# The attention layer's modulation, moved into the phase that reads out and projects the recurrence

## The reference

```python
for i in range(DEPTH_2):                                    # two layers
    last = i == DEPTH_2 - 1
    mod_x = jax.nn.silu(c) @ mod_w[i] + mod_b[i]            # [1024] @ [1024, 3072]
    mod_c = jax.nn.silu(c_ctx) @ mod_w[i] + mod_b[i]
    sh_x, sc_x, g_x = jnp.split(mod_x[:, None, :], 3, axis=-1)
    sh_c, sc_c, g_c = jnp.split(mod_c, 3, axis=-1)
    h_x = rmsnorm_2(x, norm_g[i]) * (1.0 + sc_x) + sh_x
    h_c = rmsnorm_2(ctx, norm_g[i]) * (1.0 + sc_c) + sh_c
    ...                                                     # i = 0: recurrence; i = 1: attention
    x = x + g_x * d_x
    if not last:
        ctx = ctx + g_c * d_c
```

## Time and profile before

| | us |
|---|---|
| median of three runs | 3451.7 (3448.46 to 3469.91) |
| profiled execution, own time | 3456.56 |
| its span in the trace | 3454.8 |
| TensorE busy | 2627.6 (76% of the span) |
| VectorE busy | 1449.8 (42%) |
| ScalarE busy | 705.3 (20%) |
| GpSimd busy | 499.7 (14%) |

### The profile page before, as it was taken

How to read it: one execution, slowest core, us unless ns; L and a number is a source line. 1 busy time by engine, 2 the same in 40 slices (tenths; PEclk the granted TensorE clock), 3 DMA queues, 4 the chain that set the end, 5 groups by cost and what they waited for, 6 DMA issues and landing times. The chain is left out here.

```text
span 3454.8 us, 49188 instructions
## 1 busy us (share of the span) xinstructions
PE 2627.6 (76%) x19847; PEld 1493.6 (43%) x19847; DVE 1449.8 (42%) x2794; ACT 705.3 (20%) x1317; POOL 499.7 (14%) x469
## 2 busy tenths in 40 slices
PE   5998853975777778766059999778885877888876
PEld 2542333934322333222035565367774325444542
DVE  1634666524211111111578796845554801134431
ACT  2111420101100000000025541122222112133330
POOL 0000141300211111111000000021111210044440
PEclk7999876986899989888579999989997988999998
DMA  5104501014599999888534546243433442011002
GB/s 208 67 32 146 195 8 25 6 49 162 184 415 410 414 403 415 346 336 335 226 89 124 152 123 207 75 113 112 115 104 129 159 147 81 13 23 19 8 1 79
DMA packets 337449, 540.07 MB, mean 156 GB/s; under 512 B 151685, under 2 KB 225311, under 8 KB 304081
## 3 DMA queue, kind: packets, MB, share of 16 engines
q1 hardware_dynamic: 306657, 436.31, 35.7%
q10 hardware_dynamic: 17568, 75.51, 5.4%
q0 software_dynamic: 13008, 25.20, 2.0%
HBM read 481.30 MB, written 75.02 MB: 161 GB/s over the span
## 5 line engine op out<-in xcount | busy, mean ns | idle before, releaser
L1812 PE MATMUL psum<-ex_w,hT 128*64 128x512 f32 x1344 | 348.4, 677 | 109.8 <-DMA ex_w<-in_exp_w_up 103.8
L1812 PEld LDWEIGHTS psum<-ex_w,hT 128*64 128x64 f32 x1344 | 120.0, 156 | 333.6 <-issue 325.2
L3692 POOL TENSOR_SCALAR at_p<-at_p,at_stats 128x768 f32<-128x768 f32 x64 | 139.8, 2207 | 200.8 <-DVE at_stats L3717 200.8
L533 PE MATMUL psum<-hT,weights 128*128 128x512 f32 x384 | 166.8, 592 | 0.0
L2027 DVE COPY slot_act_t<-psum 128x256 f32<-128x256 f32 x32 | 13.6, 424 | 355.0 <-PE psum L1820 355.0
L1828 PE MATMUL psum<-ex_w,slot_act_t 128*64 128x512 f32 x672 | 153.5, 598 | 7.6 <-DVE slot_act_t L2173 6.4
L234 PE MATMUL psum<-mod_ring,mod_silu 128*64 128x512 f32 x384 | 99.4, 665 | 57.6 <-DMA mod_ring<-in_w_mod 37.4
L478 PE MATMUL psum<-const,norm_xn 128*128 128x128 f32 x176 | 31.5, 343 | 126.0 <-DVE norm_xn L453 126.0
L3604 PE MATMUL psum<-mla_kT,at_qT 128*128 128x512 f32 (+1 forms) x256 | 93.8, 510 | 27.4 <-ACT at_p L3667 23.2
L2915 PE MATMUL psum<-rs_r_ident,rs_b 64*32 64x96 f32 x1536 | 89.0, 260 | 32.5 <-DVE rs_k_ident L3051 20.2
L533 PEld LDWEIGHTS psum<-hT,weights 128*128 128x128 f32 x384 | 73.0, 190 | 86.7 <-issue 86.1
(11 more groups left out here) (522 smaller groups left out, 5180.8 us busy)
## 6 DMA issues: line engine op xcount, KB each, us to landing
ex_w<-in_exp_w_gate SPq DMA_DIRECT2D x86, 1024.0 KB, 11.8
ex_w<-in_exp_w_up SPq DMA_DIRECT2D x86, 1024.0 KB, 19.3
ex_w<-in_exp_w_down ACTq DMA_DIRECT2D x60, 1024.0 KB, 15.1
ex_w<-in_exp_w_down SPq DMA_DIRECT2D x26, 1024.0 KB, 16.2
mod_ring<-in_w_mod SPq DMA_DIRECT2D x12, 2048.0 KB, 13.2
mod_ring<-in_mod_w SPq DMA_DIRECT2D x12, 2048.0 KB, 11.5
scratch_features<-tokens SPq DMA_DIRECT2D x96, 256.0 KB, 3.7
weights<-in_w_in SPq DMA_DIRECT2D x6, 2048.0 KB, 7.9
```

The costliest lines, as they stand in the source:

```text
L533: mm = pe.matmul(K.bank[2 * (f % 4)][:, :], K.wring[:, n % RING, k, m * P:(m + 1) * P], K.hT[:, k, TC:TT], start=(k == 0), stop=(k == KD - 1))
L1812: mm = pe.matmul(bank[at:at + n, :], XT[:, k, at:at + n], W[:, 0:2, k * DE:(k + 1) * DE], start=(k == 0), stop=(k == KD - 1))
L3692: pool.tensor_scalar(Pm[:, u, :], Pm[:, u, :], st[:, 3, u:u + 1], None, ALU.mult).then_inc(S["norm_done"], 1)
```

## The change

`second_modulation` is gone as a phase, and all that it did stands inside `rwkv_readout`. SyncE loads the vectors before load(0), the first weight block behind the projection's weights, and the bias and blocks 1 and 2 behind the gate rows, all before load(2); blocks 3, 4 and 5 follow load(2), load(3) and load(4). TensorE makes `part(j)` and `sum(j - 1)` between turn(j + 1) and project(j, 1). ScalarE takes evac(j) and to_row(j - 1) between its half of the copy and the square of norm(j + 2). GpSimd adds the bias of block j - 1 behind the bonus term of tile j. The partial sums use PSUM banks 6 and 7 in place of 4 and 5, and the spread gate uses 2 and 3, behind the last sums.

```diff
@@ rwkv_readout, sync @@
+            vectors_in(sp, I, vec, S["vec_in"])
             load(0)
 ...
             load(1)
             sp.dma_start(wb[:, :, :], I["rwkv_w_out_2"][0].rearrange("(k p) n -> p k n", p=P)).then_inc(S["w_in"], 16)
+            M.load(sp, 0)
             sp.dma_start(K.X[:, :, :], tokens.rearrange("(j p) n -> p j n", p=P)).then_inc(S["x_in"], 16)
             for r in range(2):
                 sp.dma_start(K.gate[:, r, :], gate_rows[r].partition_broadcast(P)).then_inc(S["x_in"], 16)
+            M.load_bias(sp)
+            M.load(sp, 1)
+            M.load(sp, 2)
             for j in range(2, NT):
                 load(j)
+                if j < 5:
+                    M.load(sp, j + 1)
@@ gpsimd @@
+            pool.memset(silu[:, :, :], 0.0).then_inc(S["vec_zero"], 1)
+            broadcast_rows(pool, sel, (S["sel_a"], S["sel_set"]))
             pool.wait_ge(S["params_in"], 32)
 ...
                 pool.tensor_tensor(v, v, b[:, :], ALU.add).then_inc(S["shifted"], 1)
+                if j == 1:
+                    pool.wait_ge(S["m_bias"], 16 * M.N)
+                if j:
+                    M.add_bias_of(pool, j - 1)
+            M.add_bias_of(pool, NT - 1)
@@ tensor @@
+            pe.wait_ge(S["silu_done"], 1)
             turn(0)
             pe.wait_ge(S["w_in"], 16)
             for j in range(NT):
                 project(j, 0)
                 if j + 1 < NT:
                     turn(j + 1)
+                M.part(pe, j)
+                if j:
+                    M.sum(pe, j - 1)
                 project(j, 1)
+            M.sum(pe, NT - 1)
+            pe.wait_ge(S["m_row"], 4)
+            columns_mm(pe, K, K.bank[0], M.row, (0, D)).then_inc(S["c_mm"], 1)
+            pe.wait_ge(S["sel_set"], 1)
+            pe.wait_ge(S["m_row"], M.N)
+            pe.wait_ge(S["gated"], 2 * NT - 2)
+            for h in range(2):
+                pe.matmul(K.bank[2 + h][:, :], sel[:, 0, :], M.row[0:2, 2 * D + h * 512:2 * D + (h + 1) * 512],
+                          start=True, stop=True).then_inc(S["wide_mm"], 1)
@@ scalar @@
+            act.wait_ge(S["vec_in"], 64)
+            act.wait_ge(S["vec_zero"], 1)
+            act.activation(silu[:, :, 0:2], vec[:, 2:4, :].rearrange("p r k -> p k r"), ACT.Silu).then_inc(S["silu_done"], 1)
             norm(0)
             copy_in(0)
             norm(1)
             for j in range(NT):
                 if j + 1 < NT:
                     copy_in(j + 1)
+                M.evac(act, j)
+                if j:
+                    M.to_row(act, j - 1)
                 if j + 2 < NT:
                     norm(j + 2)
+            M.to_row(act, NT - 1)
+            act.wait_ge(S["gated"], 2 * NT)
+            for h in range(2):
+                act.wait_ge(S["wide_mm"], h + 1)
+                act.activation(K.gate[:, 0, h * 512:(h + 1) * 512], K.bank[2 + h][:, :], ACT.Copy).then_inc(S["wide_out"], 1)
@@ vector @@
+            dve.wait_ge(S["c_mm"], 1)
+            gain = K.colA[:, WHERE_A["norm_g_2"] + KD:WHERE_A["norm_g_2"] + 2 * KD]
+            columns_out(dve, K.bank[0], gain, K.mods[:, 0, 1, :, :], K.mods[:, 0, 0, :, :], S["c_out"])
@@ mla_layer @@
-    second_modulation(K, I, 1)
```

More of the change, by code:

```diff
@@ L242, in evac, with add_bias_of @@
         act.activation(self.sums[:, c % 2, :], self.K.bank[self.parts][:, :], ACT.Copy).then_inc(self.S["m_evac"], 1)
+    def add_bias_of(self, pool, c):
+        pool.wait_ge(self.S["m_evac"], c + 1)
+        own = self.sums[0:2, c % 2, :]
+        pool.tensor_tensor(own, own, self.row[0:2, c * WCH:(c + 1) * WCH], ALU.add).then_inc(self.S["m_added"], 1)
     def add_bias(self, pool):
@@ L246, in add_bias @@
         for c in range(self.N):
-            pool.wait_ge(self.S["m_evac"], c + 1)
-            own = self.sums[0:2, c % 2, :]
-            pool.tensor_tensor(own, own, self.row[0:2, c * WCH:(c + 1) * WCH], ALU.add).then_inc(self.S["m_added"], 1)
+            self.add_bias_of(pool, c)
     def sum(self, pe, c):
@@ L3125, in rwkv_readout @@
     names = ("params_in w_in x_in in_y0 in_y1 in_bg0 in_bg1 scaled shifted v centred sq_done summed rms_done normed turned "
-             "out_a out_b mm_done gated added")
+             "out_a out_b mm_done gated added vec_in vec_zero silu_done sel_a sel_set c_mm c_out wide_mm wide_out" + Stream.NAMES)
     with ExitStack() as c, phase(nc, names) as (block, S):
@@ L3137, in rwkv_readout @@
         in_y, in_bg = (S["in_y0"], S["in_y1"]), (S["in_bg0"], S["in_bg1"])
+        vec, silu, sel = buf("mod_vec", [P, 4, KD]), buf("mod_silu", [P, KD, 64]), buf("row_selector", [2, 2, P])
+        M = Stream(K, S, buf, [(silu, I["mod_w_2"][1], I["mod_b_2"][1], n) for n in range(6)], (6, 7))
         T_, M_ = (0, 1), ((2, 3), (4, 5))
@@ L3291, in _ @@
             sp.wait_ge(S["x_in"], 16)
[L3294 to L3351, removed]
```

## The result

Over eight runs each the changed kernel took 3437.26 us (median; 3427.65 to 3440.06) and the kernel before 3454.19 (3448.46 to 3469.91). The ratio is 0.9939, with a 95% interval of 0.9923 to 0.9954. That is 21 us less (16 to 27 by the interval; the two medians alone lie 17 apart), where 20.4 were forecast. It lies within 1%, and clear of no change. The median is 6 us above the 3431.3 of the forecast; 2.5 of that is the kernel before, which took 3454.19 here and not the 3451.7 that the forecast started from.

The account below looks back on a forecast made before the run. Transfers bound the modulation, one 2 MB block every 5.4 us; VectorE paces the readout's middle. Next phase 19.1 us earlier plus 1.3 for the table makes 20.4 off 3451.7: 3431.3 us, range 3420 to 3446.

Parts of the forecast that it names:

- Opening: Start of the readout: four vector loads ahead of load(0) in SyncE's queue shift everything by 1.8 us.
- Load(2): Readout's tile 2: three weight blocks ahead in the queue, 16.2 us, make turn(2) start 14.2 us later.
- Restart: TensorE behind the wait for load(2): slowed once by a low clock, 3.0 us, from 2.7 to 3.2.
- rival (c): From turn(2) on, TensorE's clock restarts at each tile; gain gone at mean clock 0.83, 3463 us at 0.75; chance 0.05.
- Middle: Readout's tile loops: TensorE becomes the bound at 19.5 us a loop; turn(5) comes 22.1 us later.
- Rival (a): Chain over ScalarE and GpSimd delays the norms, three loops losing 2 to 4 us each; about 3442 us, chance 0.22.
- End: From turn(5) to the readout's last product: 21.65 us plus 9.1 for two parts and sums, 30.8 in all.
- tail: Behind the last product: new sum, columns, spread and last copy, hidden by nothing; 7.2 to 9.05 us, taken as 8.3.
- Table: Next phase, between squares and root: the activation table load of 1.28 us goes.
- Passage: From the last gate copy into the next phase's first square: 1.67 us, left in any case.
- (b): Loads hurt less: load(2) late by one block only, turn(2) at 2713.9 to 2717; gain 29 to 35 us, chance 0.10.
- (d): The move hides nothing: each tile longer by 3.65 + 5.4 us waiting for its block; gain 0 to 5, chance 0.06.

Follow-up runs that it names:

- the filled gap: Changed kernel plus 13 products with unused results in TensorE's wait for load(2); stretch 178.90 us against the changed kernel's 181.40, gain 2.5.
- one block only: Changed kernel without the loads of blocks 1 to 5, every part multiplying block 0; stretch 170.58 us against 181.40, gain 10.8.

## Why the prediction was right

Opening: 1.8 us of shift forecast; project(0, 0) came 1.6 later and VectorE's first pass 0.75, so the small loads cost less than their time in the queue; the runs do not show where they were hidden. Load(2): y usable at 57.6 us from the first load by the sum (3 x 5.4 behind a full ring), measured 58.1. Norm(2) 13.0 forecast, 13.6 measured; turn(2) 14.2 later forecast, 15.3 measured. The Trainium skill, "DMA: Bandwidth & Descriptors", section "Queues, rings and completion order", says that descriptors of one ring are consumed in ring order. The trace agrees: with blocks 1 and 2 behind it, load(2) was usable 10.6 us earlier, which is two blocks of 5.3.

Restart: 3.0 forecast, 2.75 measured (22.09 against 19.34), and shown to be the clock's by the filled gap. The prediction took the granted clock of 0.56 in the modulation's first 7 us for half the time at the lower level. Between levels of 0.5 and 1 it is nearly all of it; the 3.0 came from the lengths of the rows and stands. The Trainium skill, "TensorE: Matmul & The Clock Gate", section "HAM oscillation", describes a kernel whose waits for data, longer than the matmuls between them, return the clock to its lower level each time. The trace agrees for the one long wait (12.95 us, and 0.50 behind it). The rival (c), a restart in each tile, did not occur: the mean granted clock from turn(2) on was 0.97, and TensorE was left no gap.

Middle: 19.5 per loop forecast, 19.34 measured, with TensorE the bound. Rival (a) showed itself once: the square of norm(3) started right behind evac and to_row, and VectorE stood 2.87 us before its next pass in place of 1.12. It cost nothing, as TensorE was still busy at turn(3). End: 30.8 forecast, 31.1 measured; tail 8.3 forecast, 7.5 measured, with the spread at 2.37 between its bounds. Table: 1.28 gone as said.

Passage: I kept it at 1.67 and it took 2.87. This is the one term missed, since I took the row of the old phase for a constant of the program, while the merged phase has 39 semaphores to clear. With it the sum is 19.2 us for the stretch, and 19.3 were measured. That the two agree to 0.1 us is in part luck: turn(2) came 1.2 us later than forecast, and a shorter restart, shorter loops and a tail shorter by 0.8 made it good. The terms are right to about 1 us each. Rivals (b) and (d) fall: load(2) did not overtake, and the old phase's 58.85 us went at a price of 31.9 us up to the readout's last product and a tail of 7.5.

The wait for load(2), the largest delay in the prediction's sum (14.2 us), came from an order of loads that was a free choice: two blocks in another place give 9.6 us, all of them, with the parts a tile later, 13.1.

## What to carry to other kernels

Prefetched data that is wanted late should stand in the queue behind what is wanted next: in a full ring each 2 MB block ahead cost the next tile 5.3 us, and the wait of TensorE cost its restart on top. Before merging work into a phase bound by VectorE, add up both engines' loops: here the merged one made TensorE the bound at 19.3 us a tile, so a microsecond that it waited, or was given, showed in the stretch. Count what a phase's end does, too; one clear for each semaphore was paid with every engine waiting.

## What the runs showed of the hardware

A semaphore cleared singly by SyncE cost some 0.055 us in the passage between phases (0.93, 1.68 and 2.87 us with 4, 18 and 39 clears); clearing by ranges took about 15 us off a program that executes 377 of them, and left 61.

TensorE's restart does not go by the length of the idle alone. An idle of 13 us before a turn cost 2.75 us. With load(2) first one of 3.7 cost 1.7, and with one block only one of 2.6 cost as much (turn 1.58, part 4.80). With all blocks behind load(2) one of 2.9 cost nothing (turn(1) 1.09, projection 13.90). And in the tail the granted clock fell to 0.50 with no idle at all, during or soon after the 32 small matmuls of the columns.
